# Moving half of each weight piece by 64 bytes and taking its two halves in turn

## What is computed

```python
# first block: modulation from c, gated linear attention + Fourier branch, squared-ReLU MLP
h = modulate(rmsnorm(x, norm1_g), sh1, sc1)
parts = split_proj(h @ w_in)                       # also for the 256 context tokens (k, v, decays)
...
x = x + gt1 * ((gate_fft * y_fft + gate_gla * y_gla) @ w_out)
h2 = modulate(rmsnorm(x, norm2_g), sh2, sc2)
x = x + gt2 * (square(relu(h2 @ w_mlp_in)) @ w_mlp_out)
x = rmsnorm(x, final_norm_g)
# second block: three convolution / pooling mixers and a gated MLP with a width-3 convolution
u = rms_norm(x, norm_mix_pre) @ w_in_2
...
x = x + rms_norm(concat([y_a, y_b, y_c]) @ w_out_2, norm_mix_post)
up = causal_conv(rms_norm(x, norm_ffn_pre) @ w_up_2) + bias
x = x + rms_norm((silu(gate) * val) @ w_down_2, norm_ffn_post)
```

## Time and profile before

| | us |
|---|---|
| median of 3 runs | 2590.83 |
| lowest and highest | 2590.58 to 2592.93 |
| the profiled execution | 2592.11 |
| its span, first to last instruction | 2590.3 |

### The profile page before, as it was taken

One profiled execution on the slowest core, in us unless ns is written; L12 is line 12 of the kernel. 1 busy time (PEld: TensorE's weight loads), 2 busy tenths in 40 slices (PEclk: granted clock), 3 DMA queues, 4 the chain that ended last, 5 costly groups with the idle time before them and its releaser, 6 DMA issues.

```text
span 2590.3 us, 42561 instructions
## 1 busy us (share of the span) xinstructions
PE 2537.2 (98%) x18912; PEld 2378.3 (92%) x18912; DVE 1658.1 (64%) x1999; ACT 1132.6 (44%) x1299; POOL 11.2 (0%) x24
## 2 busy tenths in 40 slices
PE   6999999999999999999999999999999999999998
PEld 3688799999998999999999999999899889988996
DVE  5366666677785755555555579776677556764775
ACT  3322565544444434434434552054455435543553
POOL 0000000000000000000000000000000000000000
PEclk8999999999999999999999999999999999999999
DMA  9976565588885755555555555454455555555553
GB/s 395 361 254 229 209 218 207 202 296 290 304 292 202 278 190 186 194 192 185 194 193 184 190 183 179 147 179 170 151 185 196 196 194 187 188 195 184 190 183 110
DMA packets 77223, 547.89 MB, mean 212 GB/s; under 512 B 8848, under 2 KB 8976, under 8 KB 12272
## 3 DMA queue, kind: packets, MB, share of 16 engines
q1 hardware_dynamic: 74304, 533.53, 57.7%
q0 software_dynamic: 2448, 11.14, 1.1%
q10 hardware_dynamic: 288, 0.50, 0.1%
HBM read 539.90 MB, written 5.24 MB: 210 GB/s over the span
## 4 chain that ended last, share of the span: by engine, by line
PE 96%; DVE 2%; ACT 1%; DMA 1%; issue 0%; SPq 0%; DVEq 0%; ACTq 0%
PE acc L289 23%; PE acc L293 22%; PE acc L291 22%; PE acc L346 5%; PE acc L309 5%; PE acc L310 5%; PE acc L311 5%; PE mp L376 1%; PE mp L309 1%; PE mp L311 1%; PE mp L310 1%; DMA raw<-in_w_mod 1%; PE mp L435 0%; PE mp L498 0%; DVE macc L420 0%; PE mp L1866 0%
## 5 line engine op out<-in xcount | busy, mean ns | idle before, releaser
L257 DVE TENSOR_TENSOR wlo<-raw,whi 128x1024 fp32r<-128x1024 f32 x773 | 934.9, 1222 | 679.4 <-ACT whi L247 677.7
L247 ACT ACTIVATE whi<-raw 128x1024 fp32r<-128x1024 f32 x773 | 812.1, 1058 | 1171.9 <-PE acc L293 873.3
L293 PE MATMUL acc<-hl,whi 128*128 128x256 f32 x3296 | 922.6, 280 | 0.0
L289 PE MATMUL acc<-hh,whi 128*128 128x256 f32 x3296 | 919.4, 279 | 0.0
L291 PE MATMUL acc<-hh,wlo 128*128 128x256 f32 x3296 | 915.2, 278 | 0.0
L289 PEld LDWEIGHTS acc<-hh,whi 128*128 128x128 f32 x3296 | 622.5, 189 | 4.6 <-issue 3.0
L293 PEld LDWEIGHTS acc<-hl,whi 128*128 128x128 f32 x3296 | 618.8, 188 | 0.0
L291 PEld LDWEIGHTS acc<-hh,wlo 128*128 128x128 f32 x3296 | 616.7, 187 | 0.5
L293 PE MATMUL acc<-ml,whi 128*128 128x256 f32 x1536 | 430.1, 280 | 0.0
L289 PE MATMUL acc<-mh,whi 128*128 128x256 f32 x1536 | 426.4, 278 | 0.0
L291 PE MATMUL acc<-mh,wlo 128*128 128x256 f32 x1536 | 426.4, 278 | 0.0
(11 more groups left out here) (319 smaller groups left out, 2181.4 us busy)
## 6 DMA issues: line engine op xcount, KB each, us to landing
raw<-in_w_in SPq DMA_DIRECT2D x98, 1024.0 KB, 4.9
raw<-in_w_mod SPq DMA_DIRECT2D x96, 1024.0 KB, 5.8
raw<-in_w_up SPq DMA_DIRECT2D x88, 1024.0 KB, 4.9
raw<-in_w_mlp_in SPq DMA_DIRECT2D x64, 1024.0 KB, 4.9
raw<-in_w_mlp_out SPq DMA_DIRECT2D x64, 1024.0 KB, 4.9
raw<-in_w_down SPq DMA_DIRECT2D x44, 1024.0 KB, 4.9
raw<-in_w_out SPq DMA_DIRECT2D x32, 1024.0 KB, 4.9
raw<-in_w_fourier_out SPq DMA_DIRECT2D x8, 1024.0 KB, 5.7
```

The source lines that it names most:

```text
L247: nc.scalar.activation(whi[:, r, :], raw_slot(k)[:, 2 * GC * j:2 * GC * (j + 1)], ACT.Copy)\
L257: nc.vector.tensor_tensor(wlo[:, r, :], raw_slot(k)[:, 2 * GC * j:2 * GC * (j + 1)], whi[:, r, :].bitcast(f32), ALU.subtract).then_inc(S[" ...
L289: nc.tensor.matmul(dst, whi[:, r, cols], hi[:, kt, :], start=begin, stop=False, skip_group_check=True)
L293: last = nc.tensor.matmul(dst, whi[:, r, cols], lo[:, kt, :], start=False, stop=kt == nkt - 1, skip_group_check=True)
```

## The change

The two halves of a piece (two rows of 512 columns, or four of 256) are no longer adjacent in `whi` and `wlo`: the second begins 16 numbers, 64 bytes, further on. A place of the ring takes `SLOTW` = 1040 numbers, 4160 bytes. Both buffers grow by 256 bytes, and `region_a` is held 128 bytes shorter. ScalarE and VectorE write both halves in one instruction with an operand of two runs (`both_halves`; for the last place it is laid out from 64 bytes ahead so that it stays within the buffer). `wcols` finds the columns for PE.

In `feature_piece` the loop over column groups becomes the outer one, and inside it the triples of the first and the second half alternate: in places 0 and 2 of the ring the first half comes first, in places 1 and 3 the second. The flags for the first and last matmul of an accumulation follow. `token_piece` and the `lr` piece keep their order and only read from the new places.

```diff
--- before.py
+++ after.py
@@ -7,6 +7,7 @@
 NT = 256
 KT = D // P
 GC = 512
+GAP = 16
 NSLOT = 4
 MODS = 6
 HEADS, DK, DV = 4, 128, 256
@@ -75,6 +76,9 @@
               [8, 9, 14, 15], [10, 11, 16, 17], [0, 1, 2, 3], [4, 5]]
 
 
+SLOTW = 2 * GC + GAP
+
+
 def late_groups(p):
 
     return max(0, STREAM[:PIECE[p - 1][0]].count("m") - EARLY) // 4
@@ -111,8 +115,8 @@
 
 
         raw = sb("raw", [P, NSLOT, 4 * GC])
-        whi = sb("whi", [P, 8 * GC + 16], f32r)[:, 4:8 * GC + 4].rearrange("p (r n) -> p r n", r=4)
-        wlo = sb("wlo", [P, 8 * GC + 16], f32r)[:, 4:8 * GC + 4].rearrange("p (r n) -> p r n", r=4)
+        whi = sb("whi", [P, 4 * SLOTW + 16], f32r)
+        wlo = sb("wlo", [P, 4 * SLOTW + 16], f32r)
         tmp = sb("tmp", [P, 2, 4 * NT])
         (mrow, cv, posc, macc, stage, _, posc2, sx, post) = overlay(
             "region_s", 8192,
@@ -141,7 +145,7 @@
             [("hh", [P, KT, NT], f32r), ("hl", [P, KT, NT], f32r)],
             [("xN", [P, 2, D], f32), ("gN", [P, 2, D], f32)])
         (ch, cl, sqx, sqc, lab, keb, tq, state, dft, smid, mh, ml, _, dh, dl, hf) = overlay(
-            "region_a", 32768 + 512,
+            "region_a", 32768 + 384,
             [("ch", [P, KT, NT], f32r), ("cl", [P, KT, NT], f32r)],
             [("sqx", [P, KT, NT], f32), ("sqc", [P, KT, NT], f32)],
             [("lab", [P, 2, KEYW], f32), ("keb", [P, 2, KEYW], f32), ("tq", [P, 2, KEYW], f32),
@@ -237,6 +241,21 @@
         def raw_slot(k):
             return raw[:, RING[k], :] if RING[k] < NSLOT else raw2[:, RING[k] - NSLOT, :]
 
+        def raw_halves(k, j):
+            return raw_slot(k)[:, 2 * GC * j:2 * GC * (j + 1)].rearrange("p (a n) -> p a n", a=2)
+
+        def both_halves(w, r):
+
+            at = 4 + r * SLOTW
+            skip = GAP if r == 3 else 0
+            pair = w[:, at - skip:at - skip + 2 * (GC + GAP)].rearrange("p (a n) -> p a n", a=2)
+            return pair[:, :, skip:skip + GC]
+
+        def wcols(w, r, c, n):
+
+            at = 4 + r * SLOTW + c + (GAP if c >= GC else 0)
+            return w[:, at:at + n]
+
         def hi_piece(act, st):
             k, j = PIECE[st.p]
             r = st.p % 4
@@ -244,7 +263,7 @@
                 slot_in(act, k)
             if st.p >= 4:
                 act.wait_ge(S["used"], st.p - 3)
-            nc.scalar.activation(whi[:, r, :], raw_slot(k)[:, 2 * GC * j:2 * GC * (j + 1)], ACT.Copy)\
+            nc.scalar.activation(both_halves(whi, r), raw_halves(k, j), ACT.Copy)\
                 .then_inc(S["hi_n"], 1)
             st.p += 1
 
@@ -254,8 +273,8 @@
                 mod_acc(dve, st)
             r = st.p % 4
             dve.wait_ge(S["hi_n"], st.p + 1)
-            nc.vector.tensor_tensor(wlo[:, r, :], raw_slot(k)[:, 2 * GC * j:2 * GC * (j + 1)],
-                                    whi[:, r, :].bitcast(f32), ALU.subtract).then_inc(S["lo_n"], 1)
+            nc.vector.tensor_tensor(both_halves(wlo, r), raw_halves(k, j),
+                                    both_halves(whi, r).bitcast(f32), ALU.subtract).then_inc(S["lo_n"], 1)
             st.p += 1
 
         def conv_hi(act, st, n=8, met=None):
@@ -280,18 +299,20 @@
 
             r = st.p % 4
             pe.wait_ge(S["lo_n"], st.p + 1)
-            for k in range(2 * GC // w):
-                kt = k0 + k
-                for t in range(w // P):
-                    dst = acc[i][:, t * NT:(t + 1) * NT]
-                    cols = slice(k * w + t * P, k * w + (t + 1) * P)
-                    begin = kt == 0 and t % 2 == 0
-                    nc.tensor.matmul(dst, whi[:, r, cols], hi[:, kt, :], start=begin, stop=False,
-                                     skip_group_check=True)
-                    nc.tensor.matmul(dst, wlo[:, r, cols], hi[:, kt, :], start=False, stop=False,
-                                     skip_group_check=True)
-                    last = nc.tensor.matmul(dst, whi[:, r, cols], lo[:, kt, :], start=False,
-                                            stop=kt == nkt - 1, skip_group_check=True)
+            rows = 2 * GC // w
+            for t in range(w // P):
+                for a in range(rows // 2):
+                    for k in ((a, a + rows // 2), (a + rows // 2, a))[r % 2]:
+                        kt, c = k0 + k, k * w + t * P
+                        dst = acc[i][:, t * NT:(t + 1) * NT]
+                        begin = k0 == 0 and t % 2 == 0 and a == 0 and (k == a) == (r % 2 == 0)
+                        end = k0 + rows == nkt and a == rows // 2 - 1 and (k == a) == (r % 2 == 1)
+                        nc.tensor.matmul(dst, wcols(whi, r, c, P), hi[:, kt, :], start=begin, stop=False,
+                                         skip_group_check=True)
+                        nc.tensor.matmul(dst, wcols(wlo, r, c, P), hi[:, kt, :], start=False, stop=False,
+                                         skip_group_check=True)
+                        last = nc.tensor.matmul(dst, wcols(whi, r, c, P), lo[:, kt, :], start=False,
+                                                stop=end, skip_group_check=True)
             last.then_inc(S["used"], 1)
             st.p += 1
 
@@ -303,12 +324,12 @@
             r = st.p % 4
             pe.wait_ge(S["lo_n"], st.p + 1)
             for k in range(2):
-                kt, cols = k0 + k, slice(k * GC, (k + 1) * GC)
+                kt, c = k0 + k, k * GC
                 for bank, off, hi, lo, t0 in outs:
                     dst = bank[:, off:off + GC]
-                    nc.tensor.matmul(dst, hi[:, kt, t0:t0 + P], whi[:, r, cols], start=kt == 0, stop=False)
-                    nc.tensor.matmul(dst, hi[:, kt, t0:t0 + P], wlo[:, r, cols], start=False, stop=False)
-                    last = nc.tensor.matmul(dst, lo[:, kt, t0:t0 + P], whi[:, r, cols], start=False,
+                    nc.tensor.matmul(dst, hi[:, kt, t0:t0 + P], wcols(whi, r, c, GC), start=kt == 0, stop=False)
+                    nc.tensor.matmul(dst, hi[:, kt, t0:t0 + P], wcols(wlo, r, c, GC), start=False, stop=False)
+                    last = nc.tensor.matmul(dst, lo[:, kt, t0:t0 + P], wcols(whi, r, c, GC), start=False,
                                             stop=kt == nkt - 1)
             last.then_inc(S["used"], 1)
             st.p += 1
@@ -355,12 +376,12 @@
             r = st.p % 4
             pe.wait_ge(S["lo_n"], st.p + 1)
             for kt in range(KT):
-                cols = slice(kt * LRW, (kt + 1) * LRW)
+                c = kt * LRW
                 for x, (hi, lo) in enumerate(((hh, hl), (ch, cl))):
                     dst = acc[i][0:LRW, x * GC:x * GC + NT]
-                    nc.tensor.matmul(dst, whi[:, r, cols], hi[:, kt, :], start=kt == 0, stop=False)
-                    nc.tensor.matmul(dst, whi[:, r, cols], lo[:, kt, :], start=False, stop=False)
-                    last = nc.tensor.matmul(dst, wlo[:, r, cols], hi[:, kt, :], start=False, stop=kt == KT - 1)
+                    nc.tensor.matmul(dst, wcols(whi, r, c, LRW), hi[:, kt, :], start=kt == 0, stop=False)
+                    nc.tensor.matmul(dst, wcols(whi, r, c, LRW), lo[:, kt, :], start=False, stop=False)
+                    last = nc.tensor.matmul(dst, wcols(wlo, r, c, LRW), hi[:, kt, :], start=False, stop=kt == KT - 1)
             last.then_inc(S["used"], 1)
             st.p += 1
 
```

## The result

The changed kernel takes 2625.27 us, the median of four runs (2622.72 to 2626.2), against 2590.7 us (2589.92 to 2592.93): a ratio of 1.0127, 95% interval 1.0113 to 1.0142. It is 34 us slower; 2565 us had been forecast. The profiled execution's span is 2620.9 us instead of 2590.3, at nearly the same mean clock (0.994; before 0.993).

The account below looks back on a forecast made before the run. TensorE's matmul steps were taken as the bound; -24.5 and -1.5 us, the other parts 0, took the profiled 2592.1 us to 2566.1, on the median's scale 2565 us. Own range 2550 to 2572, whole range up to 2620.

Parts of the forecast that it names:

- What bounds the kernel: TensorE from 574 us on: time is the number of matmuls times the step between starts, 346.7 ns a feature triple.
- Part 1: Feature triples: with no load repeating a place, the step between triples falls from 119.2 to 113.8 ns; -24.5 us.
- Part 2: Stretch from 526 to 571 us: 128 feature triples at 353.5 ns would get three steps of 113.8; -1.5 us.
- Part 3: New order of triples in feature pieces: same matmuls and semaphores on PE, no wait added; 0.
- Part 4: Token pieces: moving operand now at changing places; 7 us either way possible, taken as 0.
- Part 5: ScalarE's copy to `whi` and VectorE's subtraction, now with operands of two runs, stay covered; 0.
- Second rhythm: Feature triples without the long step settle at the slower 353.5 ns: 2622 us; chance 0.29, including a part of it.
- PSUM columns: The long step comes from changing PSUM columns, changes halve: 12 us gained, 2579 us; chance 0.09, including another part gain.
- Nothing: Step hangs on the moving operand's return, cost moves within the triple, or pages' rule holds: 2591 us; chance 0.13.

Follow-up runs that it names:

- e4_low_weights_last: The kernel before with the second and third matmul of a feature triple exchanged, low weights by high activations last: 2607.68 us, ratio 1.0064.
- e2_place: The changed kernel with the old loops in `feature_piece`, so only the places differ from the kernel before: 2613.6 us, ratio 1.0082.
- e1_order: The changed kernel with every address put back, so only the order of triples differs from the kernel before: 2592.92 us, ratio 0.9999.
- e5_pad256: The kernel before with 256 unused bytes behind `wlo`, moving the activations and all other buffers behind it: 2591.59 us, ratio 0.9996.
- e8_far256: The changed kernel, same order and buffer sizes, with weights put back to the old distances from the activations modulo 256 bytes: 2595.35 us, ratio 1.0004.
- e5: Four kernels: the kernel before with 64, 128, 192 or 256 unused bytes behind `wlo`: 2611.88, 2633.67, 2621.85 and 2591.59 us.
- e5_pad128: The kernel before with 128 unused bytes behind `wlo`, moving the activations and all other buffers behind it: 2633.67 us, ratio 1.0150.
- e10_token_place: The kernel before with only the activations of the down projection (`dh`, `dl`) moved 32 bytes further on: 2590.58 us, ratio 0.9992.

## Why the prediction was wrong

**What bounds the kernel** was read rightly: the waits are the same, and the 34 us are 4538 triples by 7.5 ns.

**Part 1, the price of the places, is the step that failed**, with the wrong sign. It was right in one half. In the fast rhythm the 119 ns do belong to a load that repeats the last one's place; `e4_low_weights_last` shows it, and in the changed kernel no step stands out any more. What failed is "I take -24.5: the row nearest to a load that changes place is that of the two steps that do so now". These two steps are 113.8 ns only in the fast rhythm, and that needs a certain distance to the moving operand, which the change took from three quarters of the loads; there a load that changes place takes 118 ns as well (changed kernel: steps of 117.8, 118.6 and 117.8 ns), and the triple 354.2 ns instead of the 341.4 forecast. The prediction looked at the loads' places among themselves, modulo 128, and never at the third address in play. The sum with measured terms: in the old order the four distances occur equally often, so the mean of 346.8, 351.5, 353.2 and 353.5 is 351.3 ns, 4.6 x 4538 = 21 us, and `e2_place` measured 21 us. The changed kernel takes 34 us, 12 more than `e2_place`. There the distance changes from triple to triple rather than from half to half. That the order, harmless alone, costs 12 us on top of the places is measured; why mixing distances is worse than their mean stays open.

**Part 2** (-1.5 us) fell with part 1: from 526 to 571 us the changed kernel has 354.2 ns a triple (starts in the trace). The fast rhythm is possible in that stretch, but at the old distances: `e1_order` has 347.3 ns there and `e5_pad256` 346.9. **Part 3** held: `e1_order`, 0 within 0.1%. **Part 4**: taken as 0. The changed kernel's token triples take 59.8 / 86 = 695 ns instead of 698, about 1 us over 352 triples:

```profile
L332 PE MATMUL acc<-whi,dl x87: 387/393/399, 2059.9 to 2119.7; 128*128 128x512 f32 x87
```

**Part 5** held: 1057 and 1223 ns, and no wait of PE on a piece of the ring.

**The rivals.** "Second rhythm" had the right sign and nearly the time, 2622 us, and the rows it rested on the earlier trace rows were the ones to follow: they had shown steps of 117.8 ns for loads that change place. Its mechanism was half right, and that its number came so near is in part luck: the changed kernel does not run in the even rhythm of rows 8 (durations 278/278/278) but in an irregular one (277/280/286). The rhythm is not kept up by the repeated place (in `e1_order`, `e5_pad256` and `e8_far256` it is there in two orders, in `e4_low_weights_last` with the repetition elsewhere), but by the distances of `whi` and `wlo` to the moving operand; and even at the right ones it is only one of two, as the earlier trace rows and `e4_low_weights_last` show. What decides between the two is not known. The range ended at 2620 us, within this case rather than beyond it, and so missed. "PSUM columns" is refuted by `e1_order`. "Nothing" is refuted too: the `e5` kernels change nothing but where the buffers behind `wlo` stand, and three of them take 18 to 40 us more. The rule that the prediction cites for it, "SBUF — State Buffer" of the Trainium skill, section "SBUF: two separate sides", is that PE never waits on anyone. Drawn out as the prediction did, to mean that 64 bytes can't change anything, it doesn't agree with these runs. The traces do not say whether it is TensorE's two reads that get in each other's way or something else.

## What to carry to other kernels

Where fp32r matmuls follow each other closely, the place of the weights relative to the moving operand, modulo 256 bytes, was a parameter of this kernel worth up to 1.6% of the whole (346.8 against 351 to 355 ns a triple, in places 360), and a change of a buffer's size between them changes it unless it is a multiple of 256 bytes. When an address is moved, list all operands that are read at the same time and their distances, not only the one that is meant to change. If one step of a repeating pattern is longer than the others, look for a stretch in which the same pattern runs at another pace. If there is one, as in the earlier trace rows, a short step belongs to its rhythm, and its time can't be put for one step alone.

## What the runs showed of the hardware

- A stream of matmuls of 128 x 256 in fp32r, with a weight load each, settles into a steady rhythm that depends on the distance of weights and moving operand. The period seen is 256 bytes: 256 bytes give 346.8 ns for three, as 0 bytes do, and 64, 128 and 192 give 351.5, 353.2 and 353.5.
- 32 bytes matter (353.8 ns), and cost more than 64 (351.5).
- Moving weights and activations together by 128 bytes changes nothing (346.5 ns).
- A weight load that repeats the last one's place makes the long step at one distance (119 ns of 346.9, `e4_low_weights_last`) and the short one at another (114.1 ns of 353.2, `e5_pad128`).
- At one and the same distance there can be two rhythms, 346.9 and 353.3 ns in `e4_low_weights_last`, each kept for a hundred microseconds and more.
- With a stationary operand of activations and 512 moving weight columns, three matmuls took 698, 695, 687 or 686 ns by the distance, and at one distance (`e10_token_place`) 693 and later 687.
